# FFN-in units: one of four weight sums moves from VectorE to GpSimd, and its product moves among the plain up tiles

## The chip, the cores and the metric

The kernel runs on 1 core of one Trainium2 chip. The metric is the device time in microseconds (us) of that core, the median of several executions of the same program.

## The reference

One decoder layer on x of 256 tokens by 2048 features, all in float32. The first and the last of its three parts are SwiGLU feed-forward blocks, and the change touches only their input projection:

```
x = x + 0.5 * swiglu_ffn(rmsnorm(x, ffn1_norm), ffn1_w_in, ffn1_w_out)
x = x + concat(attention_A, attention_B) @ w_out        # token mixer, not touched
x = x + 0.5 * swiglu_ffn(rmsnorm(x, ffn2_norm), ffn2_w_in, ffn2_w_out)

def swiglu_ffn(x, w_in, w_out):
    gate, up = jnp.split(x @ w_in, 2, axis=-1)      # w_in: 2048 x 11008, D_FF = 5504
    return (jax.nn.silu(gate) * up) @ w_out
```

## The kernel before

**Tiling.** The input projection of each feed-forward block is cut into 11 units of output columns, ten of 512 gate and 512 up columns and a last one of 384 of each (`UNIT_W`). Unit 0 of each block is computed plainly (`plain_unit`). The other ten of each block, so 20 in all, run `unit(u, j)`; the change touches these and what feeds them.

**What a unit computes.** The 16 row tiles of the weights are used in two ways. Rows 0 to 7 are multiplied plainly: two row tiles are a "half", 128 x 1024 numbers, and the halves are named G0 and G1 (gate) and U0, U1 (up). Rows 8 to 15 of gate and up are handled as a 2 x 2 block product in Strassen-Winograd form: seven products, each of two halves, instead of eight. Four of the seven take their weights from the raw pieces (B11, B21, and so on), and sums of pieces are needed for T1, T3, T2 and T4. The matching sums of the inputs are made once per block in `form_sums`. A product goes into one of four PSUM banks Y, V, Z, X.

**Hi and lo.** Float32 precision is reached with three reduced-precision products: each half of weights is copied by ScalarE (ACT) into `whi`, rounded, and VectorE (DVE) writes the remainder, source minus `whi`, into `wlo`. This pair of steps is `split` (L835 on ACT, L1173 on DVE). TensorE (PE) then runs hi x hi, hi x lo, lo x hi. `whi` and `wlo` are rings of `SLOTS` = 4 halves: ACT may write half h only when PE has used half h - 4 (`weights_used`), DVE may write `wlo` of h when `whi` of h is there (`weights_hi`), and PE starts h when `wlo` of h is there (`weights_lo`).

**Order.** Each engine goes through a list written out by hand. PE's order in a unit is T1, B11, eight transposes of the unit before (`act_turn`), G0, T2, B21, T3, G1, B22, T4, U0, U1; a form product is 2 halves of 6 matmuls, a plain piece 2 halves of 12. The constants `T1, B11, ... U0` are the places of these halves in the unit (22 halves), and U0 stood for all four plain up halves.

**Buffers.** `raw` has 6 slots of 4 row tiles (128 x 2048), filled by one DMA each on SyncE's queue, which waits in order for the slot to come free (`free`, wait on L370). `tsum` is one buffer of the same size. Before the change DVE made four sums in a unit: `sum_t1` (L1335) and `sum_t3` (L1342) near the end of the unit before, `sum_t2` (L1349) over the B11 piece, and `sum_t4` (L1355) into `tsum`, just after the remainder of B21's first half.

**GpSimd (POOL)** only makes a few constants, some small powers (`x_power`, L464, and L495) and a few DMAs.

Of the kernel before, what the change touches and what calls it, by code (L numbers as in the profile page):

```python
# [32 lines left out]
UNITS = -(-D_FF // W)  # L33
# [9 lines left out]

T1, B11, G0, T2, B21, T3, G1, B22, T4, U0 = 0, 2, 4, 6, 8, 10, 12, 14, 16, 18
UNIT_HALVES = 22
# [62 lines left out]
IN_P, OUT_P = [0, 0], [0, 0]  # L108
# [45 lines left out]
def layer(nc, io, out):  # L154
# [3 lines left out]
    with ctx:  # L158
# [144 lines left out]
        def kept(u, g):  # L303
# [19 lines left out]
        xg_ready, s_summed, s_hi, s_ready = (sem(n) for n in ("xg_ready", "s_summed", "s_hi", "s_ready"))  # L323
        sums_done, copied, w_done, gate_added, c11_done = (
            sem(n) for n in ("sums_done", "copied", "w_done", "gate_added", "c11_done"))
        sq_done, hss_ready, hms_ready, hr_ready, hsc_ready, qn_ready, qk_psum, qkT_ready, v_ready = (
# [16 lines left out]
        def _(sp):  # L343
            def free(n):
                for u in range(2):
                    if IN_P[u] <= n < OUT_P[u]:
                        j, i = (n - IN_P[u]) // 8, (n - IN_P[u]) % 8
                        if j == 0:
                            return weights_lo, IN[u] + 2 * i + 2
                        if i == LOAD["B11"]:  # L350
                            return sums_done, 4 * ((UNITS - 1) * u + j)
                        last = {LOAD["B21"]: B21, LOAD["B12"]: T3, LOAD["B22"]: B22, LOAD["G0"]: G0, LOAD["G1"]: G1, LOAD["U0"]: U0, LOAD["U1"]: U0 + 2}[i]
# [97 lines left out]
        def _(pool):  # L450
# [35 lines left out]
            for m in range(2 * GROUPS):  # L486
# [8 lines left out]
                pool.tensor_tensor(hr[:], hms[:], neg_half[:].rearrange("p (b i) -> p b i", b=TB), ALU.pow).then_inc(hr_ready, 1)  # L495
            x_power(2)

        @block.tensor
        def _(pe):
# [87 lines left out]
            def unit(u, j):  # L587
# [238 lines left out]
        def _(act_e):  # L826
# [139 lines left out]
            def unit(u, j):  # L966
                Y, V, Z, X = unit_banks(j)
                base, n, w, s = unit_half(u, j), IN_P[u] + 8 * j, UNIT_W[j], j % 2
                first, w2 = (UNITS - 1) * u + j - 1, 2 * w
                act_e.wait_ge(sums_done, 4 * first + 1)  # L970
                for i in range(2):
# [11 lines left out]
                A(p1s[:, 0:w], Y[:, 0:w], ACT.Copy).then_inc(copied, 1)  # L983
                act_e.wait_ge(sums_done, 4 * first + 3)
                for i in range(2):
                    split(base + T2 + i, piece_half(n + LOAD["B11"], i, w2), w2)
                loaded(n + LOAD["B21"])
# [12 lines left out]
                act_copy(u, j - 1)  # L1000
                act_e.wait_ge(sums_done, 4 * first + 4)
                for i in range(2):
                    split(base + T4 + i, tsum[:, i * w2:(i + 1) * w2], w2)
                loaded(n + LOAD["U0"])
                for i in range(2):
                    split(base + U0 + i, piece_half(n + LOAD["U0"], i, w2), w2)
                loaded(n + LOAD["U1"])
                split(base + U0 + 2, piece_half(n + LOAD["U1"], 0, w2), w2)
                silu(u, j)
                split(base + U0 + 3, piece_half(n + LOAD["U1"], 1, w2), w2)  # L1010

# [156 lines left out]
        def _(dve):  # L1168
# [23 lines left out]
            def form_sums(u):  # L1192
                dve.wait_ge(xg_ready, u + 1)
                A11, A21, A12, A22 = xg[:, 0:4, 0:P], xg[:, 0:4, P:2 * P], xg[:, 4:8, 0:P], xg[:, 4:8, P:2 * P]
                V.tensor_tensor(A22, A21, A22, ALU.add).then_inc(s_summed, 1)
# [4 lines left out]
                V.tensor_tensor(A12, A12, A11, ALU.subtract).then_inc(s_summed, 1)  # L1200

# [127 lines left out]
            def sum_t1(u, j):  # L1329
# [3 lines left out]
                if j > 1:  # L1333
                    dve.wait_ge(weights_lo, unit_half(u, j - 1) + T4 + 2)
                V.tensor_tensor(tsum[:, 0:4 * w], whole(n + LOAD["B12"], w), whole(n + LOAD["B11"], w),  # L1335
                                ALU.subtract).then_inc(sums_done, 1)

            def sum_t3(u, j):
                n, w = IN_P[u] + 8 * j, UNIT_W[j]
                full(n + LOAD["B22"])  # L1340
                dve.wait_ge(sums_done, 4 * ((UNITS - 1) * u + j - 1) + 1)
                V.tensor_tensor(whole(n + LOAD["B12"], w), whole(n + LOAD["B22"], w), whole(n + LOAD["B12"], w),  # L1342
                                ALU.subtract).then_inc(sums_done, 1)

            def sum_t2(u, j):
                n, w = IN_P[u] + 8 * j, UNIT_W[j]
                dve.wait_ge(sums_done, 4 * ((UNITS - 1) * u + j - 1) + 2)
                dve.wait_ge(weights_lo, unit_half(u, j) + B11 + 2)
                V.tensor_tensor(whole(n + LOAD["B11"], w), whole(n + LOAD["B12"], w), whole(n + LOAD["B11"], w),  # L1349
                                ALU.add).then_inc(sums_done, 1)  # L1350

            def sum_t4(u, j):
                n, w = IN_P[u] + 8 * j, UNIT_W[j]
                dve.wait_ge(sums_done, 4 * ((UNITS - 1) * u + j - 1) + 3)
                V.tensor_tensor(tsum[:, 0:4 * w], whole(n + LOAD["B21"], w), whole(n + LOAD["B11"], w),  # L1355
                                ALU.subtract).then_inc(sums_done, 1)

# [32 lines left out]
            def unit(u, j):  # L1390
# [11 lines left out]
                for i in range(2):  # L1402
                    split(base + T2 + i, piece_half(n + LOAD["B11"], i, w2), w2)
# [12 lines left out]
                split(base + T4, tsum[:, 0:w2], w2)  # L1416
# [3 lines left out]
                split(base + T4 + 1, tsum[:, w2:2 * w2], w2)  # L1420
                split(base + U0, piece_half(n + LOAD["U0"], 0, w2), w2)
                dve.wait_ge(weights_used, base + B22 + 2)
                dve.wait_ge(copied, 3 * first + 3)
                V.tensor_tensor(gset[:, s, 0, 0:w], Z[:, 0:w], gset[:, s, 0, 0:w], ALU.add).then_inc(gate_added, 1)
                split(base + U0 + 1, piece_half(n + LOAD["U0"], 1, w2), w2)
                split(base + U0 + 2, piece_half(n + LOAD["U1"], 0, w2), w2)
                if j + 1 < UNITS:
                    sum_t1(u, j + 1)
                split(base + U0 + 3, piece_half(n + LOAD["U1"], 1, w2), w2)
                if j + 1 < UNITS:  # L1430
# [253 lines left out]
```

## Time and profile before

| what | value |
|---|---|
| median of 3 runs | 1762.78 us (1762.37 to 1762.95) |
| span of the profiled execution | 1760.7 us |
| PE busy | 1754.5 us |
| DVE busy | 1490.9 us |
| ACT busy | 1077.5 us |
| POOL busy | 28.1 us |
| matmuls | 8036 |

The span runs from the first to the last instruction of the profiled execution. It is 2.1 us under the median of the runs. No time of its own is shown for the profiled execution beside its span. Matmuls overlap in the record, so that PE's busy time hides waits shorter than the pipeline's own length; start-to-start distances are the surer measure.

### The profile page before, as it was taken

How to read it: one execution, taken by the hardware profiler on the slowest of the kernel's cores; microseconds unless marked ns; L12 is line 12 of the kernel's file. 1: busy time of each engine (PE TensorE's matmuls, PEld its weight loads, DVE VectorE, ACT ScalarE, POOL GpSimd, SP SyncE). 2: the span in 40 equal slices, each digit the busy share in tenths (PEclk: the TensorE clock that was granted, in tenths of full speed). 3: DMA queues.
4: the chain of work that ended last, by engine and by line, in shares of the span. 5: the costliest groups of instructions: out<-in, count | busy, mean ns of one | idle time of the engine just before them, and what ended most of it. 6: DMA issues, size and time to landing. Idle time of an engine off the chain costs nothing.

```text
span 1760.7 us, 20876 instructions
## 1 busy us (share of the span) xinstructions
PE 1754.5 (100%) x8036; PEld 1463.4 (83%) x8036; DVE 1490.9 (85%) x1627; ACT 1077.5 (61%) x1359; POOL 28.1 (2%) x34
## 2 busy tenths in 40 slices
PE   9999999999999999999999999999999999999999
PEld 7888888888988888888888888888888888988887
DVE  7999999998899998575655655999999999899998
ACT  7666666666666666454545544666666666666665
POOL 0000000000000001100000000000000000000000
PEclk9999999999999999999999999999999999999999
DMA  9655555554655556555455547355555555564762
GB/s 379 233 213 211 196 191 192 191 191 156 228 215 192 203 215 209 182 188 182 156 188 166 169 168 262 121 211 194 202 213 212 213 213 192 190 207 163 257 212 93
DMA packets 154931, 350.85 MB, mean 199 GB/s; under 512 B 5864, under 2 KB 14592, under 8 KB 154704
## 3 DMA queue, kind: packets, MB, share of 16 engines
q1 hardware_dynamic: 152288, 342.02, 54.9%
q0 software_dynamic: 1424, 5.53, 1.0%
q10 hardware_dynamic: 1120, 1.97, 0.3%
q8 instruction: 64, 1.05, 0.2%
q14 instruction: 35, 0.29, 0.0%
HBM read 347.37 MB, written 3.69 MB: 199 GB/s over the span
## 4 chain that ended last, share of the span: by engine, by line
PE 95%; DVE 2%; SPq 1%; DMA 1%; issue 0%; ACT 0%; ACTq 0%; DVEq 0%
PE bank L570 9%; PE bank L568 9%; PE bank L569 9%; PE bank L552 7%; PE bank L554 7%; PE bank L553 7%; PE bank L509 7%; PE bank L511 7%; PE bank L510 7%; PE bank L639 5%; PE bank L641 5%; PE bank L640 5%; PE bank L667 3%; PE bank L666 3%; PE bank L665 3%; PE bank L537 1%
## 5 line engine op out<-in xcount | busy, mean ns | idle before, releaser
L1173 DVE TENSOR_TENSOR wlo<-raw,whi 128x1024 fp32r<-128x1024 f32 (+1 forms) x626 | 742.1, 1205 | 176.9 <-ACT whi L835 171.8
L835 ACT ACTIVATE whi<-raw 128x1024 fp32r<-128x1024 f32 (+1 forms) x626 | 650.7, 1046 | 392.8 <-PE bank L511 188.9
L568 PE MATMUL bank<-whi,xs 128*128 128x512 f32 (+1 forms) x768 | 297.9, 388 | 0.5 <-DVE xs L1368 0.2
L570 PE MATMUL bank<-whi,xs 128*128 128x512 f32 (+1 forms) x768 | 295.5, 385 | 0.0
L569 PE MATMUL bank<-wlo,xs 128*128 128x512 f32 (+1 forms) x768 | 295.4, 385 | 0.0
L568 PEld LDWEIGHTS bank<-whi,xs 128*128 128x128 f32 x768 | 144.3, 188 | 29.0 <-DVE wlo L1365 1.1
L570 PEld LDWEIGHTS bank<-whi,xs 128*128 128x128 f32 x768 | 144.2, 188 | 27.7
L569 PEld LDWEIGHTS bank<-wlo,xs 128*128 128x128 f32 x768 | 144.4, 188 | 26.8
L639 PE MATMUL bank<-whi,aw_hi 128*128 128x512 f32 x420 | 164.0, 390 | 0.0
L641 PE MATMUL bank<-whi,aw_lo 128*128 128x512 f32 x420 | 163.5, 389 | 0.0
L640 PE MATMUL bank<-wlo,aw_hi 128*128 128x512 f32 x420 | 163.5, 389 | 0.0
L509 PE MATMUL bank<-whi,xs 128*128 128x512 f32 x384 | 155.1, 404 | 0.4 <-DVE wlo L1173 0.4
L511 PE MATMUL bank<-whi,xs 128*128 128x512 f32 x384 | 150.0, 391 | 0.0
L510 PE MATMUL bank<-wlo,xs 128*128 128x512 f32 x384 | 149.5, 389 | 0.0
L835 ACT ACTIVATE whi<-tsum 128x1024 fp32r<-128x1024 f32 (+1 forms) x80 | 83.0, 1040 | 97.8 <-PE bank L570 64.1
L552 PE MATMUL bank<-whi,sf 128*128 128x512 f32 (+1 forms) x320 | 122.8, 384 | 0.0
L554 PE MATMUL bank<-whi,sf 128*128 128x512 f32 (+1 forms) x320 | 122.8, 384 | 0.0
L553 PE MATMUL bank<-wlo,sf 128*128 128x512 f32 (+1 forms) x320 | 122.7, 384 | 0.0
L1037 ACT ACTIVATE whi<-raw 128x1024 fp32r<-128x1024 f32 x80 | 84.8, 1060 | 61.9 <-PE bank L641 38.6
L1173 DVE TENSOR_TENSOR wlo<-tsum,whi 128x1024 fp32r<-128x1024 f32 (+1 forms) x80 | 94.0, 1195 | 26.0 <-ACT whi L835 26.0
L1453 DVE TENSOR_TENSOR wlo<-raw,whi 128x1024 fp32r<-128x1024 f32 x80 | 97.1, 1220 | 1.7 <-ACT whi L1037 0.8
L639 PEld LDWEIGHTS bank<-whi,aw_hi 128*128 128x128 f32 x420 | 78.8, 188 | 17.4 <-issue 1.3
(204 smaller groups left out, 2724.7 us busy)
## 6 DMA issues: line engine op xcount, KB each, us to landing
raw<-ffn_w_in SPq DMA_DIRECT2D x158, 1024.0 KB, 7.1
raw<-ffn_w_out SPq DMA_DIRECT2D x84, 1024.0 KB, 6.7
raw<-w_in SPq DMA_DIRECT2D x48, 1024.0 KB, 5.0
raw<-w_out SPq DMA_DIRECT2D x16, 1024.0 KB, 5.0
raw<-ffn_w_in SPq DMA_DIRECT2D x16, 768.0 KB, 4.5
x<-x SPq DMA_DIRECT2D x4, 512.0 KB, 12.4
raw<-ffn_w_out SPq DMA_DIRECT2D x4, 512.0 KB, 3.8
raw<-ffn_w_in SPq DMA_DIRECT2D x3, 512.0 KB, 7.4
```

What stands on the lines that cost most here:

```text
L509: mm(banks[b][:, 0:w], stationary[:, k, 0, tok], hi, start=k == 0, stop=False, skip_group_check=True)
L510: mm(banks[b][:, 0:w], stationary[:, k, 0, tok], lo, start=False, stop=False, skip_group_check=True)
L511: last = mm(banks[b][:, 0:w], stationary[:, k, 1, tok], hi, start=False, stop=k == k_total - 1, skip_group_check=True)
L552: mm(bank_out[:, 0:w], st_hi, hi, start=start and i == 0 and k == 0, stop=False, skip_group_check=True)
L568: mm(banks[b][:, 0:w], xs[:, k + i, 0, tok], hi, start=starts[b] and k + i == 0, stop=False, skip_group_check=True)
L569: mm(banks[b][:, 0:w], xs[:, k + i, 0, tok], lo, start=False, stop=False, skip_group_check=True)
L570: last = mm(banks[b][:, 0:w], xs[:, k + i, 1, tok], hi, start=False, stop=k + i == last_k, skip_group_check=True)
L639: mm(bank_out[:], st_hi, hi, start=i == 0, stop=False, skip_group_check=True)
L640: mm(bank_out[:], st_hi, lo, start=False, stop=False, skip_group_check=True)
L641: last = mm(bank_out[:], st_lo, hi, start=False, stop=k == FT - 1, skip_group_check=True)
L835: A(whi[:, h % SLOTS, 0:n_el], src, ACT.Copy).then_inc(weights_hi, 1)
L1173: V.tensor_tensor(wlo[:, h % SLOTS, 0:n_el], src, whi[:, h % SLOTS, 0:n_el].bitcast(f32), ALU.subtract).then_inc(weights_lo, 1)
```

## The change

`sum_t4` is gone from DVE. GpSimd makes the same sum with a new function `add_b21`: it waits until DVE has written the remainder of B21's second half, and then adds the raw B21 piece onto `tsum` in place (128 x 2048 float32, two inputs in SBUF), which now holds T2 at that time: `sum_t2` writes into `tsum` instead of over the B11 piece, and the T2 halves are split from there. ACT waits for `t4_added` before it copies T4. The T4 product and its splits move behind the first two plain up halves (U0) and ahead of the last two (U1). The B11 slot comes free after `sum_t2`, the B21 slot after the add. For T4 to be a plain addition, some signs are turned in the sums of inputs, the sums of weights and in two additions onto PSUM banks; the number and shape of those instructions stay.

```diff
-T1, B11, G0, T2, B21, T3, G1, B22, T4, U0 = 0, 2, 4, 6, 8, 10, 12, 14, 16, 18
+T1, B11, G0, T2, B21, T3, G1, B22, U0, T4, U1 = 0, 2, 4, 6, 8, 10, 12, 14, 16, 18, 20
...
                         if i == LOAD["B11"]:
-                            return sums_done, 4 * ((UNITS - 1) * u + j)
+                            return sums_done, 3 * ((UNITS - 1) * u + j)
+                        if i == LOAD["B21"]:
+                            return t4_added, (UNITS - 1) * u + j
...
+            def add_b21(u, j):
+                n = 4 * UNIT_W[j]
+                pool.wait_ge(weights_lo, unit_half(u, j) + B21 + 2)
+                pool.tensor_tensor(tsum[:, 0:n], tsum[:, 0:n], raw[:, raw_slot(IN_P[u] + 8 * j + LOAD["B21"]), 0:n],
+                                   ALU.add).then_inc(t4_added, 1)
+
+            for j in range(1, UNITS):
+                add_b21(0, j)
...
             x_power(2)
+            for j in range(1, UNITS):
+                add_b21(1, j)
...
         # PE, unit
                 pe.wait_ge(w_done, first + 1)
+                for i in range(2):
+                    plain(base + U0 + i, 2 * i, (V, Y), (False, False), w, -1)
                 form(base + T4, Y, lambda k, t: xs[:, 12 + k, t, blk1], w, False)
-                for i in range(4):
-                    plain(base + U0 + i, 2 * i, (V, Y), (False, False), w, 7)
+                for i in range(2):
+                    plain(base + U1 + i, 4 + 2 * i, (V, Y), (False, False), w, 7)
...
         # ACT, unit
-                act_e.wait_ge(sums_done, 4 * first + 4)
+                loaded(n + LOAD["U0"])
+                for i in range(2):
+                    split(base + U0 + i, piece_half(n + LOAD["U0"], i, w2), w2)
+                act_e.wait_ge(t4_added, first + 1)
                 for i in range(2):
                     split(base + T4 + i, tsum[:, i * w2:(i + 1) * w2], w2)
...
         # DVE
-                V.tensor_tensor(whole(n + LOAD["B11"], w), whole(n + LOAD["B12"], w), whole(n + LOAD["B11"], w),
+                V.tensor_tensor(tsum[:, 0:4 * w], whole(n + LOAD["B12"], w), whole(n + LOAD["B11"], w),
                                 ALU.add).then_inc(sums_done, 1)
-
-            def sum_t4(u, j):
-                n, w = IN_P[u] + 8 * j, UNIT_W[j]
-                dve.wait_ge(sums_done, 4 * ((UNITS - 1) * u + j - 1) + 3)
-                V.tensor_tensor(tsum[:, 0:4 * w], whole(n + LOAD["B21"], w), whole(n + LOAD["B11"], w),
-                                ALU.subtract).then_inc(sums_done, 1)
...
                 split(base + B21, piece_half(n + LOAD["B21"], 0, w2), w2)
-                sum_t4(u, j)
                 split(base + B21 + 1, piece_half(n + LOAD["B21"], 1, w2), w2)
...
-                V.tensor_tensor(gset[:, s, 1, 0:w], Y[:, 0:w], gset[:, s, 1, 0:w], ALU.add).then_inc(w_done, 1)
+                V.tensor_tensor(gset[:, s, 1, 0:w], gset[:, s, 1, 0:w], Y[:, 0:w], ALU.subtract).then_inc(w_done, 1)
```

## Rows read from the trace of the kernel before

**Rows 1.** The page's busy times, share of the span, instructions.
```profile
PE 1754.5 (100%) x8036; PEld 1463.4 (83%) x8036; DVE 1490.9 (85%) x1627; ACT 1077.5 (61%) x1359; POOL 28.1 (2%) x34
```

**Rows 2.** Windows of one unit each: busy us per engine, TensorE clock, DMA share.
```profile
69.40:111.12 41.72, 41.72 (x190) 34.61 (x189) 38.56 (x33) 26.80 (x30) 0.00 (x0) 1.00 0.57 203
...
361.40:403.10 41.70, 41.70 (x190) 34.62 (x189) 38.50 (x33) 26.81 (x30) 0.00 (x0) 1.00 0.56 202
```

**Rows 3.** Timeline of PE in one unit: start us, duration us, instruction.
```profile
278.38 0.39 PE L552 MATMUL bank<-whi,sf 128*128 128x512 f32 x1
...
279.74 0.39 PE L552 MATMUL bank<-whi,sf 128*128 128x512 f32 x1
...
294.70 0.39 PE L568 MATMUL bank<-whi,xs 128*128 128x512 f32 x1
...
302.86 0.39 PE L552 MATMUL bank<-whi,sf 128*128 128x512 f32 x1
```

**Rows 4.** Timeline of DVE in the same unit.
```profile
267.86 4.94 DVE L1173 TENSOR_TENSOR wlo<-raw,whi 128x1024 fp32r<-128x1024 f32 x4
272.72 2.28 DVE L1355 TENSOR_TENSOR tsum<-raw 128x2048 f32<-128x2048 f32 x1
274.92 2.35 DVE L1173 TENSOR_TENSOR wlo<-raw,whi 128x1024 fp32r<-128x1024 f32 x2
277.44 3.50 DVE L1173 TENSOR_TENSOR wlo<-raw,whi 128x1024 fp32r<-128x1024 f32 x3 [0.17 <-ACT whi L835]
...
298.81 2.35 DVE L1173 TENSOR_TENSOR wlo<-tsum,whi 128x1024 fp32r<-128x1024 f32 x2
```

**Rows 5.** Timeline of ACT in the same unit.
```profile
273.14 1.06 ACT L835 ACTIVATE whi<-raw 128x1024 fp32r<-128x1024 f32 x1 [1.60 <-PE bank L570]
274.50 1.06 ACT L835 ACTIVATE whi<-raw 128x1024 fp32r<-128x1024 f32 x1 [0.29 <-PE bank L554]
```

**Rows 6.** POOL's groups by form: busy us, mean ns of one, idle before.
```profile
L455 POOL TENSOR_SCALAR_AFFINE_SELECT ident<-ident 128x128 f32<-128x128 f32 x1 | 0.3, 292 | 0.2 <-POOL ident L453 0.2
L453 POOL MEMSET ident<- 128x128 f32 x1 | 0.2, 206 | 0.0
...
L452 POOL MEMSET warm<- 128x1 f32 x1 | 0.1, 99 | 0.0
```

**Rows 7.** Timeline of POOL: three of its eleven powers.
```profile
708.57 0.72 POOL L464 TENSOR_TENSOR rstd<-xms,neg_half 128x2 f32<-128x2 f32 x1 [28.86 <-DVE xms L1211]
...
743.55 1.66 POOL L495 TENSOR_TENSOR hr<-hms,neg_half 128x8 f32<-128x8 f32 x1 [2.33 <-DVE hms L1484]
...
1112.50 1.60 POOL L464 TENSOR_TENSOR rstd<-xms,neg_half 128x2 f32<-128x2 f32 x1 [145.30 <-DVE xms L1211]
```

**Rows 8.** Timeline of DVE around these three POOL instructions.
```profile
709.70 1.23 DVE L1173 TENSOR_TENSOR wlo<-raw,whi 128x1024 fp32r<-128x1024 f32 x1 [1.22 <-ACT whi L835]
...
743.60 1.23 DVE L1173 TENSOR_TENSOR wlo<-raw,whi 128x1024 fp32r<-128x1024 f32 x1
...
1112.33 1.22 DVE L1173 TENSOR_TENSOR wlo<-raw,whi 128x1024 fp32r<-128x1024 f32 x1
```

**Rows 9.** Timelines of PE, ACT and DVE in a block's last, 384 wide unit.
```profile
442.12 0.33 PE L552 MATMUL bank<-whi,sf 128*128 128x384 f32 x1
...
438.68 0.85 ACT L835 ACTIVATE whi<-raw 128x768 fp32r<-128x768 f32 x1 [0.19 <-PE bank L554]
...
446.90 0.96 DVE L1173 TENSOR_TENSOR wlo<-tsum,whi 128x768 fp32r<-128x768 f32 x1 [0.73 <-ACT whi L835]
```

**Rows 10.** Waits of the DMA queue: us in total, times, longest us.
```profile
SPq L370 <- DVE tsum L1355: 389.8, 20, 20.5
```

**Rows 11.** Timeline of SyncE's queue: loads issued near the unit's end.
```profile
284.29 12.79 SPq L370 DMA_DIRECT2D raw<-ffn_w_in  x6
```

**Rows 12.** Timeline of PE: transposes at the start, and in a unit.
```profile
1.60 4.53 PE L517 MATMUL bank<-ident 128*128 128x128 f32 x20 [1.60 <-POOL ident L455]
...
266.58 1.04 PE L537 MATMUL bank<-ident,gset 128*128 128x128 f32 x8
```

More of the change, by code:

```diff
@@ L323, in layer @@
         xg_ready, s_summed, s_hi, s_ready = (sem(n) for n in ("xg_ready", "s_summed", "s_hi", "s_ready"))
-        sums_done, copied, w_done, gate_added, c11_done = (
-            sem(n) for n in ("sums_done", "copied", "w_done", "gate_added", "c11_done"))
+        sums_done, t4_added, copied, w_done, gate_added, c11_done = (
+            sem(n) for n in ("sums_done", "t4_added", "copied", "w_done", "gate_added", "c11_done"))
         sq_done, hss_ready, hms_ready, hr_ready, hsc_ready, qn_ready, qk_psum, qkT_ready, v_ready = (
@@ L350, in free @@
                         if i == LOAD["B11"]:
-                            return sums_done, 4 * ((UNITS - 1) * u + j)
-                        last = {LOAD["B21"]: B21, LOAD["B12"]: T3, LOAD["B22"]: B22, LOAD["G0"]: G0, LOAD["G1"]: G1, LOAD["U0"]: U0, LOAD["U1"]: U0 + 2}[i]
+                            return sums_done, 3 * ((UNITS - 1) * u + j)
+                        if i == LOAD["B21"]:
+                            return t4_added, (UNITS - 1) * u + j
+                        last = {LOAD["B12"]: T3, LOAD["B22"]: B22, LOAD["G0"]: G0, LOAD["G1"]: G1, LOAD["U0"]: U0, LOAD["U1"]: U1}[i]
                         return weights_lo, unit_half(u, j) + last + 2
@@ L969, in unit @@
                 first, w2 = (UNITS - 1) * u + j - 1, 2 * w
-                act_e.wait_ge(sums_done, 4 * first + 1)
+                act_e.wait_ge(sums_done, 3 * first + 1)
                 for i in range(2):
@@ L983, in unit @@
                 A(p1s[:, 0:w], Y[:, 0:w], ACT.Copy).then_inc(copied, 1)
-                act_e.wait_ge(sums_done, 4 * first + 3)
+                act_e.wait_ge(sums_done, 3 * first + 3)
                 for i in range(2):
-                    split(base + T2 + i, piece_half(n + LOAD["B11"], i, w2), w2)
+                    split(base + T2 + i, tsum[:, i * w2:(i + 1) * w2], w2)
                 loaded(n + LOAD["B21"])
@@ L1000, in unit @@
                 act_copy(u, j - 1)
-                act_e.wait_ge(sums_done, 4 * first + 4)
-                for i in range(2):
-                    split(base + T4 + i, tsum[:, i * w2:(i + 1) * w2], w2)
                 loaded(n + LOAD["U0"])
@@ L1006, in unit @@
                     split(base + U0 + i, piece_half(n + LOAD["U0"], i, w2), w2)
+                act_e.wait_ge(t4_added, first + 1)
+                for i in range(2):
+                    split(base + T4 + i, tsum[:, i * w2:(i + 1) * w2], w2)
                 loaded(n + LOAD["U1"])
-                split(base + U0 + 2, piece_half(n + LOAD["U1"], 0, w2), w2)
+                split(base + U1, piece_half(n + LOAD["U1"], 0, w2), w2)
                 silu(u, j)
-                split(base + U0 + 3, piece_half(n + LOAD["U1"], 1, w2), w2)
+                split(base + U1 + 1, piece_half(n + LOAD["U1"], 1, w2), w2)
             def ffn_out(u):
@@ L1194, in form_sums @@
                 A11, A21, A12, A22 = xg[:, 0:4, 0:P], xg[:, 0:4, P:2 * P], xg[:, 4:8, 0:P], xg[:, 4:8, P:2 * P]
-                V.tensor_tensor(A22, A21, A22, ALU.add).then_inc(s_summed, 1)
+                V.tensor_tensor(A22, A21, A22, ALU.subtract).then_inc(s_summed, 1)
                 dve.wait_ge(s_summed, 4 * u + 1)
@@ L1199, in form_sums @@
                 dve.wait_ge(s_summed, 4 * u + 3)
-                V.tensor_tensor(A12, A12, A11, ALU.subtract).then_inc(s_summed, 1)
+                V.tensor_tensor(A12, A12, A11, ALU.add).then_inc(s_summed, 1)
             def form_splits(u):
@@ L1335, in sum_t1 @@
                 V.tensor_tensor(tsum[:, 0:4 * w], whole(n + LOAD["B12"], w), whole(n + LOAD["B11"], w),
-                                ALU.subtract).then_inc(sums_done, 1)
+                                ALU.add).then_inc(sums_done, 1)
             def sum_t3(u, j):
@@ L1340, in sum_t3 @@
                 full(n + LOAD["B22"])
-                dve.wait_ge(sums_done, 4 * ((UNITS - 1) * u + j - 1) + 1)
+                dve.wait_ge(sums_done, 3 * ((UNITS - 1) * u + j - 1) + 1)
                 V.tensor_tensor(whole(n + LOAD["B12"], w), whole(n + LOAD["B22"], w), whole(n + LOAD["B12"], w),
-                                ALU.subtract).then_inc(sums_done, 1)
+                                ALU.add).then_inc(sums_done, 1)
             def sum_t2(u, j):
                 n, w = IN_P[u] + 8 * j, UNIT_W[j]
-                dve.wait_ge(sums_done, 4 * ((UNITS - 1) * u + j - 1) + 2)
+                dve.wait_ge(sums_done, 3 * ((UNITS - 1) * u + j - 1) + 2)
                 dve.wait_ge(weights_lo, unit_half(u, j) + B11 + 2)
-                V.tensor_tensor(whole(n + LOAD["B11"], w), whole(n + LOAD["B12"], w), whole(n + LOAD["B11"], w),
+                V.tensor_tensor(tsum[:, 0:4 * w], whole(n + LOAD["B12"], w), whole(n + LOAD["B11"], w),
                                 ALU.add).then_inc(sums_done, 1)
-            def sum_t4(u, j):
-                n, w = IN_P[u] + 8 * j, UNIT_W[j]
-                dve.wait_ge(sums_done, 4 * ((UNITS - 1) * u + j - 1) + 3)
-                V.tensor_tensor(tsum[:, 0:4 * w], whole(n + LOAD["B21"], w), whole(n + LOAD["B11"], w),
-                                ALU.subtract).then_inc(sums_done, 1)
             def plain_unit(u):
@@ L1402, in unit @@
                 for i in range(2):
-                    split(base + T2 + i, piece_half(n + LOAD["B11"], i, w2), w2)
+                    split(base + T2 + i, tsum[:, i * w2:(i + 1) * w2], w2)
                 split(base + B21, piece_half(n + LOAD["B21"], 0, w2), w2)
-                sum_t4(u, j)
                 split(base + B21 + 1, piece_half(n + LOAD["B21"], 1, w2), w2)
@@ L1412, in unit @@
                 dve.wait_ge(copied, 3 * first + 1)
-                V.tensor_tensor(gset[:, s, 1, 0:w], Y[:, 0:w], gset[:, s, 1, 0:w], ALU.add).then_inc(w_done, 1)
+                V.tensor_tensor(gset[:, s, 1, 0:w], gset[:, s, 1, 0:w], Y[:, 0:w], ALU.subtract).then_inc(w_done, 1)
                 for i in range(2):
                     split(base + B22 + i, piece_half(n + LOAD["B22"], i, w2), w2)
-                split(base + T4, tsum[:, 0:w2], w2)
+                split(base + U0, piece_half(n + LOAD["U0"], 0, w2), w2)
                 dve.wait_ge(weights_used, base + G1 + 2)
@@ L1419, in unit @@
                 V.tensor_tensor(gset[:, s, 1, 0:w], X[:, 0:w], gset[:, s, 1, 0:w], ALU.add).then_inc(gate_added, 1)
-                split(base + T4 + 1, tsum[:, w2:2 * w2], w2)
-                split(base + U0, piece_half(n + LOAD["U0"], 0, w2), w2)
+                split(base + U0 + 1, piece_half(n + LOAD["U0"], 1, w2), w2)
+                split(base + T4, tsum[:, 0:w2], w2)
                 dve.wait_ge(weights_used, base + B22 + 2)
                 dve.wait_ge(copied, 3 * first + 3)
-                V.tensor_tensor(gset[:, s, 0, 0:w], Z[:, 0:w], gset[:, s, 0, 0:w], ALU.add).then_inc(gate_added, 1)
-                split(base + U0 + 1, piece_half(n + LOAD["U0"], 1, w2), w2)
-                split(base + U0 + 2, piece_half(n + LOAD["U1"], 0, w2), w2)
+                V.tensor_tensor(gset[:, s, 0, 0:w], Z[:, 0:w], gset[:, s, 0, 0:w], ALU.subtract).then_inc(gate_added, 1)
+                split(base + T4 + 1, tsum[:, w2:2 * w2], w2)
+                split(base + U1, piece_half(n + LOAD["U1"], 0, w2), w2)
                 if j + 1 < UNITS:
                     sum_t1(u, j + 1)
-                split(base + U0 + 3, piece_half(n + LOAD["U1"], 1, w2), w2)
+                split(base + U1 + 1, piece_half(n + LOAD["U1"], 1, w2), w2)
                 if j + 1 < UNITS:
```

## The prediction

> **What bounds the kernel now.** I read the page's busy times first. PE is busy for 1754.5 of 1760.7 us [rows 1]; a thing taken off another engine can win only where PE waits for it. Then the windows, one unit each: eight units in a row of 41.7 us, PE busy through all of each, granted clock 1.00 (2.4 GHz), DVE busy 38.5 and ACT 26.8 [rows 2]. Then PE's timeline in one unit: the two halves of T3 start 1.36 us apart, which is 6 matmuls of 0.227 us [rows 3], and a whole unit is 180 such matmuls (14 form halves of 6, 8 plain halves of 12) and eight transposes: 180 x 0.227 = 40.9, and 0.8 for the transposes. That is all of the 41.7 us. So PE never waits in a unit; it has nothing to win there. DVE is next, with 3.2 us idle in a unit, and what counts is how far it runs ahead of PE at each half.
>
> **How far ahead, at the place of the edit.** Before, DVE writes four remainders from 267.86, sum_t4 from 272.72 to 274.92 (in line the instructions follow 0.08 us before the shown end), the remainders of B21's second and T3's first half from 274.92, T3's second from 277.44 [rows 4]. T3's halves are due on PE at 278.38 and 279.74 [rows 3]. The first is ready at 274.92 + 2.35 = 277.3, 1.1 us early; the second at 277.44 + 1.2 = 278.65, 1.1 us early. This is the thinnest lead of the stretch, as the halves behind T3 are plain ones, for which PE takes 2.7 us and DVE 1.15.
>
> **The parts of the change.**
>
> Removed: 20 sums of 2.28 us on DVE (18 of this size and 2 of 384-wide units). PE waits for none of them, so this is worth 0 us by itself. It makes DVE earlier only up to the next wait for ACT: `whi` of B21's second half is ready at 273.14 + 1.06 = 274.20, of T3's first at 275.56, and of T3's second only when DVE's own wait for it ends, 277.44 [rows 4, 5], so DVE writes B21's second remainder from 274.23 to 275.45, T3's first from 275.59 to 276.8 and T3's second at 277.44 as before. ACT's times hang on the ring and so on PE.
>
> T2 written to `tsum`: the same instruction with another output, 0. The signs: the same instructions, 0. The B11 slot comes free earlier, after sum_t2 at 267.86 and not after sum_t4 at 274.92; the DMA queue waited 389.8 us for it in 20 units [rows 4, 10], but what it lets in is U0, and had anyone on PE's path waited for U0, units would show a gap [rows 2]; 0. The B21 slot now waits for the add; the piece that takes it goes out in the burst of loads from 284.29 on [rows 11], so an add that ends by then costs nothing.
>
> T4 moved: it is due at 294.70 instead of 289.26, as U0's two plain halves go first [rows 3]. A place in the ring behind them comes free at most 1.36 us later, one form half, for U1's first half, and with it `sum_t1` and the next unit's first remainder: this was ready at 298.81 + 1.2 = 300.0 for 302.86 [rows 3, 4], 2.9 us early, so 1.4 us are covered: 0. If the shift were more than 2.9 us, the rest would be paid 20 times.
>
> Added: an addition on POOL, 128 x 2048, two SBUF inputs. The trace has no POOL instruction of this size. Nearest rows: memset of one column 99 ns, of 128 columns 206, a select with one input over 128 columns 292 [rows 6]. A written element costs (206 - 99)/127 = 0.84 ns and an input (292 - 206)/128 = 0.67 ns more. Two inputs: 0.84 + 2 x 0.67 = 2.18 ns, times 2048, and 0.1 to start: 4.57 us. From below I take DVE's own 2.28 us for this sum [rows 4], from above two passes at the select's whole rate of 1.5 ns: 6.2 us. The powers, 0.72 and 1.66 us for 2 and 8 elements [rows 7], would give far more, but a power is computed, not moved, and I leave them out. I take 4.6. The Trainium skill, GPSIMD Engine Reference, section on performance versus the Vector engine, gives 4497 ns as measured for this very operation; by it the sum below would be 2 us smaller, as an estimate. The value itself is no problem for T4: it starts at 275.55, ends at 280.1, and T4's copy can be made once B22's first half has left the ring: 294.70 less two plain halves of 2.72 and a form half of 1.36, 287.9.
>
> What matters is DVE beside it. POOL's two-element power took 0.72 us with DVE idle until 709.70, but 1.60 us at 1112.50, when DVE had begun a remainder (two SBUF inputs) at 1112.33 that ended at 1113.55; 1113.5 + 0.6 is just its end [rows 7, 8]. So a POOL instruction that reads SBUF stood still until the DVE instruction with two SBUF inputs was over. I read this as a shared path that one holds to the end of its reading. The other order the trace shows only for a tiny read: at 743.60 DVE started 0.05 us after an eight-element POOL read and lost 0.01 us. I take it that the rule holds there too, and that the add keeps the path for its whole 4.6 us. The Trainium skill, SBUF — State Buffer, section "Who interferes with whom", says this outright: a VectorE instruction with two SBUF inputs and a GpSimd instruction that reads SBUF exclude each other, whichever starts first keeps the port pair for the whole instruction, and the other "fully blocks". The trace agrees in the one order it shows; by the rows alone, where only POOL is seen to stand, the sum could as well be 0.
>
> **Worked out for one unit.** POOL starts at about 275.55, between B21's second remainder (ends 275.45) and T3's first (hi part ready at 275.56). It holds until 275.55 + 4.57 = 280.1; T3's first remainder is then ready at 280.1 + 1.22 + 0.05 = 281.4, and PE wanted it at 278.38: 3.0 us of waiting. If DVE is first, T3's first is ready in time, POOL holds from 276.8 to 281.4, and T3's second is ready at 282.6 for 279.74: 2.9. Behind it DVE catches up at 1.15 us a half against 1.36 and then 2.7. Queued behind the held instruction on DVE are the remainders of G1 and the addition onto the Y bank; they are late by as much as PE is, so nobody waits twice. So 18 x 3.0 = 54. In the 384-wide unit T3 is due at 442.12, its hi part is ready at 439.53, the add takes 0.1 + 1536 x 2.18 = 3.45: 439.55 + 3.45 + 0.96 + 0.05 - 442.12 = 1.9 [rows 9], twice: 4. Together **+58 us** on the profiled span of 1760.7, so 1819; the runs' median is 2.1 above that span, so **1821 us**.
>
> The bounds of the add: with 2.28 us the wait is 275.55 + 2.28 + 1.27 - 278.38 = 0.7, in the narrow units 0.2, sum 13: 1776. With 6.2 us it is 4.6, narrow (4.7 us) 3.1, sum 89: 1852.
>
> **Rivals.**
>
> No change (1762.8). The path is not shared this way, or VectorE always goes first and POOL takes what is left; its sum has until 294.70 less 2.3 for the two copies of T4's first half, 292, some 16 us. For it: the eight-element read cost DVE nothing, and DVE's sums disappear. Against it: the 1.60 us row. This is the rival on the other side. The point from which it decides: a hold of DVE shorter than 278.38 - 275.55 - 1.27 = 1.55 us costs nothing, a longer one costs what it is longer.
>
> Both go at half speed while they overlap. T3's first remainder 275.6 to 277.9, its second to 280.2 (0.5 late), G1's first to 282.5 (0.9 more late): 1.4 x 20 = 27, so 1790 us. Only the 1.60 row speaks against it, which is a full stop.
>
> The clock falls after each wait. All rows of units show 1.00, but PE never waits there. At the start, after 1.6 us without work, 20 transposes take 4.53 us, 0.23 each, and in a unit eight take 1.04, 0.13 each [rows 12], so PE began at about the lower of its levels (1.2 GHz). If each new wait were followed by such a stretch, 4.5 us at half speed lose 2.2, times 20 is 45 more: about 1866. PE is idle 1.6 us there without work behind it, here 2.9 us after a full stretch; no row shows what that does.
>
> Faster would need waits of PE in the units, and the rows of units show none.
>
> **Chances.** Full stop of DVE 0.70, with its own range 1776 to 1852; half speed 0.09; no change 0.15; clock 0.04; faster 0.02. Faster by over 0.2% (3.5 us, about what a measurement of this kernel can tell from none) 0.02, within it 0.15, slower 0.83. The range holds the stop, the half speed and the lower end of the clock case (a shorter slow stretch), 0.8 in all: 1770 to 1855. It leaves out no change and faster below, and the rest of the clock case above.
>
> **What the profile will show.** POOL: 20 additions of 4.6 us (3.5 in the narrow units). DVE: one L1173 instruction a unit, just behind B21's, of over 4 us or begun over 4 us late. PE: one wait of 3.0 us a unit, for `wlo`, at T3's first or second half; units of 44.7 us. T4's copy on ACT without a wait for POOL. Wrong if units keep 41.7 us, if the add takes over 6 us, if the wait stands at T4 or T1, or if the granted clock falls under 1.00.

## The result, and the profile after

The changed kernel takes 1843.51 us (median of 4, 1837.4 to 1845.95) against 1762.72 before, a ratio of 1.0453 (95% interval 1.0441 to 1.0466): 81 us slower. Forecast were 1821 us and a range of 1770 to 1855. The span of the profiled execution is 1839.8 us, 79.1 more than before.

The page's busy times and the waits of PE (us in total, times, longest) in the changed kernel:

```profile
PE 1777.9 (97%) x8036; PEld 1473.9 (80%) x8036; DVE 1531.0 (83%) x1607; ACT 1076.3 (59%) x1359; POOL 118.4 (6%) x54
...
PE bank L565 <- DVE wlo L1188: 54.8, 20, 2.8
```

Before, PE had nowhere a wait of this kind worth a row. Now there is one in each of the 20 units, at the first matmul of a form product (L565), for a remainder of DVE. DVE has 20 instructions less (1607 for 1627) and is 40 us longer busy. Where that comes from, the groups by form and the timelines of GpSimd and DVE in one unit say:

```profile
L478 POOL TENSOR_TENSOR tsum<-tsum,raw 128x2048 f32<-128x2048 f32 x18 | 82.5, 4582 | 703.1 <-DVE wlo L1188 703.1
...
L1188 DVE TENSOR_TENSOR wlo<-raw,whi 128x1024 fp32r<-128x1024 f32 x554 | 747.6, 1363 | 228.3 <-ACT whi L850 223.3
L1188 DVE TENSOR_TENSOR wlo<-tsum,whi 128x1024 fp32r<-128x1024 f32 x108 | 128.8, 1220 | 3.5 <-ACT whi L850 3.5
...
251.89 4.58 POOL L478 TENSOR_TENSOR tsum<-tsum,raw 128x2048 f32<-128x2048 f32 x1 [43.10 <-DVE wlo L1188]
...
250.58 10.38 DVE L1188 TENSOR_TENSOR wlo<-raw,whi 128x1024 fp32r<-128x1024 f32 x5 [1.32 <-ACT whi L850]
```

GpSimd's add takes 4.58 us, where 4.57 was worked out. The mean remainder from `raw` rose from 1.22 to 1.36 us, that from `tsum` stayed. The last row holds five remainders in a row: at 1.14 us apart they would be 5.8 us long, and they are 10.4, so they are 4.6 us longer in all, as long as GpSimd's add, which begins at 251.89, just behind the first of them (250.58 + 1.22 = 251.80). PE in the same unit:

```profile
254.50 0.39 PE L567 MATMUL bank<-whi,xs 128*128 128x512 f32 x1
257.70 0.76 PE L565 MATMUL bank<-whi,sf 128*128 128x512 f32 x1 [2.81 <-DVE wlo L1188]
258.26 0.63 PE L566 MATMUL bank<-wlo,sf 128*128 128x512 f32 x1
258.69 0.63 PE L567 MATMUL bank<-whi,sf 128*128 128x512 f32 x1
...
395.16 0.47 PE L565 MATMUL bank<-whi,sf 128*128 128x512 f32 x1 [2.81 <-DVE wlo L1188]
395.47 0.40 PE L566 MATMUL bank<-wlo,sf 128*128 128x512 f32 x1
```

The next matmul was due at 254.50 + 0.23 = 254.73 and began at 257.70, 2.97 us late; this is T3's first half, where [rows 3] had no gap. Behind the wait two things can be seen. At 395.16 the matmuls go on at nearly their usual distance. Behind 257.70 they are 0.43 us apart, not 0.23. The windows from the start of one add to the start of the next, called distances from here on, and four short ones around that wait, show what it is (the last three numbers are granted clock, DMA share and GB/s):

```profile
112.93:157.77 44.84, 42.03 (x190) 34.53 (x189) 40.51 (x31) 26.78 (x30) 4.58 (x1) 1.00 0.53 187
204.21:251.89 47.68, 44.87 (x190) 36.61 (x189) 40.59 (x31) 26.77 (x30) 4.58 (x2) 0.93 0.50 176
251.89:298.05 46.16, 43.35 (x190) 35.50 (x189) 40.59 (x31) 26.78 (x30) 4.58 (x2) 0.96 0.51 182
...
256.00:258.00 2.00, 0.30 (x1) 0.33 (x2) 2.00 (x2) 0.00 (x0) 0.47 (x1) 0.77 0.00 0
258.00:259.00 1.00, 1.00 (x3) 0.81 (x3) 1.00 (x2) 0.00 (x0) 0.00 (x0) 0.50 0.00 0
259.00:260.00 1.00, 1.00 (x4) 0.71 (x4) 1.00 (x2) 0.00 (x0) 0.00 (x0) 0.50 0.31 43
260.00:261.00 1.00, 1.00 (x5) 0.82 (x4) 0.96 (x1) 0.31 (x1) 0.00 (x0) 0.75 0.72 178
```

The granted clock is at 0.50, the lower level of 1.2 GHz. Cut finer, the windows give 0.59 from 257.0 to 257.5 and 0.99 from 260.5 to 261.0: the clock fell at about 257.1, when PE had stood since 254.89, and rose at about 260.5. From 257.70 on PE worked in that stretch, at half its pace. A unit of 512 columns was 41.72 us; it is 44.84 now where the clock stays at 1.00, and mostly 46.2 to 46.5, once 47.7, where it falls. There are 18 distances inside the two blocks, 16 from one wide unit to the next and 2 that end in the narrow one (43.61 and 41.99 us). In 11 of the 18 the granted clock falls, and these are 18 us longer in sum than without it. So the 79 us are 18 x 3.12 = 56 us of waits in the wide units, 18 us of clock, and what is left, about 5, in the two narrow ones.

### The profile page after: what moved, and what is told of

Its sections match the earlier page's. It is cut to its first block, busy times and chain, and to the rows that moved or that the text cites. A ratio compares the mean times of both kernels' runs of the same rounds, so it can differ in the third digit from the quotient of the medians.

```text
span 1839.8 us, 20876 instructions
## 1 busy us (share of the span) xinstructions
PE 1777.9 (97%) x8036; PEld 1473.9 (80%) x8036; DVE 1531.0 (83%) x1607; ACT 1076.3 (59%) x1359; POOL 118.4 (6%) x54
## 3 DMA queue, kind: packets, MB, share of 16 engines
q8 instruction: 64, 1.05, 0.2%
## 4 chain that ended last, share of the span: by engine, by line
PE 91%; DVE 7%; ACT 1%; DMA 0%; issue 0%; SPq 0%; ACTq 0%; DVEq 0%
PE bank L581 9%; PE bank L582 9%; PE bank L583 9%; DVE wlo L1188 6%; PE bank L522 6%; PE bank L524 6%; PE bank L523 6%; PE bank L565 6%; PE bank L567 6%; PE bank L566 6%; PE bank L654 5%; PE bank L655 5%; PE bank L656 5%; PE bank L680 3%; PE bank L681 3%; PE bank L682 3%
## 5 line engine op out<-in xcount | busy, mean ns | idle before, releaser
L1188 DVE TENSOR_TENSOR wlo<-raw,whi 128x1024 fp32r<-128x1024 f32 (+1 forms) x586 | 783.5, 1351 | 237.8 <-ACT whi L850 232.6
L850 ACT ACTIVATE whi<-raw 128x1024 fp32r<-128x1024 f32 (+1 forms) x586 | 611.1, 1047 | 520.4 <-PE bank L583 203.3
L565 PE MATMUL bank<-whi,sf 128*128 128x512 f32 (+1 forms) x320 | 130.8, 409 | 54.8 <-DVE wlo L1188 54.8
L850 ACT ACTIVATE whi<-tsum 128x1024 fp32r<-128x1024 f32 (+1 forms) x120 | 120.6, 1036 | 50.8 <-DVE tsum L1350 20.5
L1188 DVE TENSOR_TENSOR wlo<-tsum,whi 128x1024 fp32r<-128x1024 f32 (+1 forms) x120 | 139.9, 1193 | 3.9 <-ACT whi L850 3.5
L478 POOL TENSOR_TENSOR tsum<-tsum,raw 128x2048 f32<-128x2048 f32 (+1 forms) x20 | 90.3, 4514 | 779.5 <-DVE wlo L1188 779.5
L567 PE MATMUL bank<-whi,sf 128*128 128x512 f32 (+1 forms) x320 | 129.9, 406 | 0.0
L566 PE MATMUL bank<-wlo,sf 128*128 128x512 f32 (+1 forms) x320 | 129.2, 404 | 0.0
L565 PEld LDWEIGHTS bank<-whi,sf 128*128 128x128 f32 x320 | 63.4, 198 | 74.4 <-issue 60.2
```

The lines of the kernel that those rows point to most:

```text
L565: mm(bank_out[:, 0:w], st_hi, hi, start=start and i == 0 and k == 0, stop=False, skip_group_check=True)
L850: A(whi[:, h % SLOTS, 0:n_el], src, ACT.Copy).then_inc(weights_hi, 1)
L1188: V.tensor_tensor(wlo[:, h % SLOTS, 0:n_el], src, whi[:, h % SLOTS, 0:n_el].bitcast(f32), ALU.subtract).then_inc(weights_lo, 1)
```

## The experiments

In all of them the times stand beside the kernel before on the same chip (1762.7 to 1762.9). In the code lines, "..." marks what is left out. The runs with an extra GpSimd instruction work over the B21 piece when nobody reads it any more and compute what the kernel before computes.

**All but GpSimd's add.** The changed kernel, the sum made by VectorE in its old place:

```diff
...
-            for j in range(1, UNITS):
-                add_b21(0, j)
...
+                V.tensor_tensor(tsum[:, 0:4 * w], tsum[:, 0:4 * w], whole(n + LOAD["B21"], w),
+                                ALU.add).then_inc(t4_added, 1)
...
                 split(base + B21, piece_half(n + LOAD["B21"], 0, w2), w2)
+                sum_t4(u, j)
                 split(base + B21 + 1, piece_half(n + LOAD["B21"], 1, w2), w2)
...
```

> The changed kernel in all its parts (T2 in tsum, T4 behind U0, turned signs, B11 slot freed early), only that VectorE makes the sum T2 + B21 at its old place and GpSimd makes none. Theory (the whole loss is VectorE standing still behind GpSimd's add, and the clock that falls with PE's waits): units of 41.7 us as before, granted clock 1.00, 1763 us within 2. Rival 1 (the move of T4 or the later sum of the next unit's T1 costs a wait of its own): a wait of PE at T4, U1 or T1 and more than 1767 us. Rival 2 (the early issue of U0's load disturbs): longer remainders or copies in the stretch of the load, again over 1767.

Measured: 1763.52 us, ratio 1.0004 (0.9995 to 1.0013), clock 1.00. The move of T4, T2 in `tsum`, the signs and the earlier slot cost nothing that can be measured. All of the loss belongs to having the add on GpSimd, at its place.

**Only GpSimd's add, with nobody waiting for it.**

```diff
+            def ghost(u, j):
+                b21 = raw[:, raw_slot(IN_P[u] + 8 * j + LOAD["B21"]), :]
+                pool.wait_ge(weights_lo, unit_half(u, j) + B21 + 2)
+                n = min(2048, 4 * UNIT_W[j])
+                pool.tensor_tensor(b21[:, 0:n], b21[:, 0:n], b21[:, 0:n], ALU.add).then_inc(ghost_done, 1)
...
```

> The kernel before, unchanged, with one more GpSimd addition in each of the 20 units, 128 x 2048 with two SBUF inputs, made when B21's second remainder is written, over the B21 piece, which nobody reads any more; only the slot's next load waits for it. No engine on PE's path waits for its result. Theory (VectorE is shut out of the second SBUF read path while GpSimd reads): one VectorE remainder in each unit late by up to 4.6 us, PE waits about 3.2 us in each unit (T3's second half: path held from 277.25 to 281.8, ready at 283.0, due at 279.74), 18 x 3.2 + 2 x 2 = 62 us, and up to 20 to 30 us of lower clock as in the changed kernel: 1825 to 1855. Rival (the loss comes from waiting for the sum's result, or from where T4 stands): 1763.

Measured: 1815.46 us, ratio 1.0299 (1.0285 to 1.0313). The rival, that the loss hangs on the sum's result or T4's place, is out: here nothing on PE's path waits for GpSimd. But the time lies below what I expected, 1825 at least. Distances between wide units are 43.97 us where the clock stays and 45.6 in four of the 16; a fifth fall, to 0.96 in the window, is in the first block's distance that ends in the narrow unit (42.64 us against 40.99 in the second). Without a fall PE waits 2.25 us a unit and not 3.2, so the path was held for 3.6 us (277.2 + 3.6 + 1.2 = 282.0, 2.25 after 279.74), though the record of the add says 4.51. That opened the question that the last two runs answer.

**GpSimd busy, but reading nothing.** Three memsets in place of the add:

```diff
+                for k in range(3):
+                    if k:
+                        pool.wait_ge(ghost_step, 2 * first + k)
+                    pool.memset(b21[:, 0:4 * UNIT_W[j]], 0.0).then_inc(ghost_done if k == 2 else ghost_step, 1)
...
```

> As the run with the extra addition, but GpSimd writes zeros three times over the same piece (three memsets of 128 x 2048, each about 1.8 us, so about 5.4 us of GpSimd work that writes SBUF and reads nothing). Theory (it is GpSimd's reading that shuts VectorE's second input out): no remainder is longer than 1.23 us, units of 41.7 us, 1763 within 2. Rival (any GpSimd work beside VectorE stops it, through the write path or the whole port pair): waits of PE of up to 3 us a unit, over 1800.

Measured: 1762.69 us, ratio 0.9999 (0.999 to 1.0008). The timelines of GpSimd and DVE in one unit:

```profile
234.69 5.57 POOL L482 MEMSET raw<- 128x2048 f32 x3 [36.15 <-DVE wlo L1189]
...
235.94 3.50 DVE L1189 TENSOR_TENSOR wlo<-raw,whi 128x1024 fp32r<-128x1024 f32 x3 [0.16 <-ACT whi L851]
```

5.6 us of GpSimd's writing, and three remainders within it take 3.50 us as in [rows 4]. So it is GpSimd's reading that shuts VectorE out. The memsets write to the place to which the extra add writes, so the write and its address are not what counts; whether the address of what is read does, was not tried.

**A short add.** The extra addition once more, cut down:

```diff
-                n = min(2048, 4 * UNIT_W[j])
+                n = min(512, 4 * UNIT_W[j])
```

> As the run with the extra addition, but only 128 x 512, so that GpSimd reads for about 1.2 us. Theory (what counts is how far the hold exceeds VectorE's lead over PE): the path is held from about 277.25 to 278.45, T3's second remainder is ready at 279.7 for 279.74, so no wait or under 0.1 us: 1763 to 1765. Rival (each collision costs a fixed restart, whatever the size): more than 1770.

Measured: 1763.40 us, ratio 1.0002 (0.9993 to 1.0011). The collision is there, the three remainders take 4.09 us and not 3.50:

```profile
236.15 4.09 DVE L1186 TENSOR_TENSOR wlo<-raw,whi 128x1024 fp32r<-128x1024 f32 x3 [0.16 <-ACT whi L848]
```

A hold of about 1 us at a place where DVE is 1.1 us ahead costs nothing; there is no fixed price per collision.

**VectorE late, GpSimd idle.** The real sum moved behind B21's second remainder, and one more sum behind it:

```diff
...
+                V.tensor_tensor(tsum[:, 0:4 * w], tsum[:, 0:4 * w], whole(n + LOAD["B21"], w),
+                                ALU.add).then_inc(t4_added, 1)
+                dve.wait_ge(t4_added, 2 * ((UNITS - 1) * u + j - 1) + 1)
+                V.tensor_tensor(whole(n + LOAD["B21"], w), whole(n + LOAD["B21"], w), whole(n + LOAD["B22"], w),
+                                ALU.add).then_inc(t4_added, 1)
...
                 split(base + B21 + 1, piece_half(n + LOAD["B21"], 1, w2), w2)
+                sum_t4(u, j)
...
```

> The changed kernel with GpSimd idle: VectorE makes the sum T2 + B21 itself, but only after B21's second remainder, and behind it one more sum of 128 x 2048 over the dead B21 piece, so that T3's first remainder starts about 4.4 us late, as behind GpSimd's add. Question: is the loss beyond 3 us a unit, the lower granted clock, a thing of PE's waiting or of GpSimd's work? Theory (PE's wait of about 3 us lets the clock fall in some units): PE waits 2.8 us a unit, clock 0.5 for some us behind the wait in about half of the units, 54 us of waits and 10 to 25 of clock, 1827 to 1843. Rival (the clock falls because of GpSimd's add): units of 44.5 us all through, clock 1.00, 1818.

Measured: 1842.77 us, ratio 1.0454 (1.0435 to 1.0472), within the spread of the changed kernel itself. Two windows of one unit each:

```profile
158.37:203.11 44.74, 42.01 (x189) 34.55 (x189) 40.52 (x35) 26.78 (x30) 0.00 (x0) 1.00 0.52 189
294.89:341.20 46.31, 43.58 (x189) 35.68 (x188) 40.60 (x34) 26.79 (x30) 0.00 (x0) 0.96 0.50 182
```

With GpSimd at 0.00 the units are 44.7 us, 3.0 more than before, and in 11 of 18 distances the clock falls, to 0.96 or less in the window, as often as in the changed kernel. So the clock falls behind PE's waits whoever makes PE wait, and the rival, that GpSimd's work lowers it, is out.

**Half as late.** The same without the extra sum:

```diff
                 split(base + B21 + 1, piece_half(n + LOAD["B21"], 1, w2), w2)
+                sum_t4(u, j)
```

> As the run with VectorE late and GpSimd idle, but with the real sum alone behind B21's second remainder and no second one, so that T3's first remainder starts 2.2 us late instead of 4.4. Theory (PE waits for what exceeds VectorE's lead, and a short wait leaves the clock): ready at 275.45 + 2.2 + 1.2 = 278.9 for 278.38, 0.5 us a unit, 10 us, clock 1.00: 1773 (1768 to 1776). Rival (any wait at this place costs clock too): over 1780 and a granted clock under 0.99 in windows of some units.

Measured: 1776.94 us, ratio 1.0080 (1.0065 to 1.0095); units of 42.4 us, the wide ones all within 0.06 us of each other, clock 1.00. The wait is 0.7 us and not the expected 0.5, so the time is 1 us over the expected range; the wait costs just itself, 14 us. The rival, that any wait at this place costs clock too, is out. The sum costs these 14 us by its place alone: on the same engine, one remainder earlier, it is free (1763.52).

**The real add in four slices.**

```diff
...
-                pool.wait_ge(weights_lo, unit_half(u, j) + B21 + 2)
-                pool.tensor_tensor(tsum[:, 0:n], tsum[:, 0:n], raw[:, raw_slot(IN_P[u] + 8 * j + LOAD["B21"]), 0:n],
-                                   ALU.add).then_inc(t4_added, 1)
...
+                for k, h in enumerate((B21 + 2, G1 + 1, G1 + 2, B22 + 2)):
+                    part = slice(k * w, (k + 1) * w)
+                    pool.wait_ge(weights_lo, unit_half(u, j) + h)
+                    pool.tensor_tensor(tsum[:, part], tsum[:, part], b21[:, part], ALU.add).then_inc(t4_added, 1)
...
```

> The changed kernel with the same real sum on GpSimd cut into four additions of 128 x 512, each let go by another remainder of VectorE (B21's second, G1's first and second, B22's second). Each holds the read path about 1.2 us, and VectorE's lead at these places is 1.5, 2.9, 3.4 and about 1.8 us. Theory (a hold shorter than the lead costs nothing): no wait of PE, 1763 to 1765. Rival (the added holds pile up, 4.9 us in a unit in which VectorE has only 5.4 us idle): 10 us and more above, with waits at T3, G1 or T1.

Measured: 1763.56 us, ratio 1.0005 (0.9996 to 1.0014). Same sum, same engine, same amount of reading, and no wait of PE behind it. The first row is the window of one unit, the second and third are VectorE and GpSimd in it:

```profile
238.88:280.63 41.75, 41.75 (x190) 34.62 (x189) 38.76 (x32) 26.80 (x30) 7.97 (x5) 1.00 0.55 202
...
240.53 5.03 DVE L1190 TENSOR_TENSOR wlo<-raw,whi 128x1024 fp32r<-128x1024 f32 x3
...
275.90 1.29 POOL L481 TENSOR_TENSOR tsum<-tsum,raw 128x512 f32<-128x512 f32 x1 [29.18 <-DVE wlo L1190]
```

VectorE stands here too: its three remainders take 5.03 us and not 3.50, in pieces that its lead over PE covers. A slice's own work is about 1.2 us, as in the one record of 1.29 us; the other three records of a unit are some 2.2 us, with the slice's own standing behind VectorE in them.

It repairs the change but does not win over the kernel before, since PE is busy through the unit in both.

**The whole add, later.**

```diff
-                pool.wait_ge(weights_lo, unit_half(u, j) + B21 + 2)
+                pool.wait_ge(weights_lo, unit_half(u, j) + G1 + 2)
```

> The changed kernel with one edit: GpSimd's add waits for G1's second remainder instead of B21's second. It then holds the path from 281.05 to 285.65 in the unit's time, over the addition onto the Y bank (one input in PSUM, should not be held) and B22's first remainder, ready then at 286.9 for 286.54. Theory: PE waits about 0.4 us a unit at B22's first half, 8 us in all, clock 1.00, 1771 (1766 to 1775). If the addition with one input in PSUM is held too, it starts 4 us late, without cost for PE. Rival (the add costs its 4.6 us of VectorE wherever it stands): over 1800.

Measured: 1783.39 us, ratio 1.0118 (1.0102 to 1.0133): far below the changed kernel, but 20 us above the one before, 12 more than I had worked out. GpSimd and DVE in one unit, and from the list of waits the one that is new:

```profile
202.83 4.63 POOL L478 TENSOR_TENSOR tsum<-tsum,raw 128x2048 f32<-128x2048 f32 x1 [39.05 <-DVE wlo L1188]
...
203.12 0.69 DVE L1421 TENSOR_TENSOR gset<-gset,bank 128x512 f32<-128x512 f32 x1 [0.37 <-PE bank L567]
203.72 7.08 DVE L1188 TENSOR_TENSOR wlo<-raw,whi 128x1024 fp32r<-128x1024 f32 x3
...
DVE tsum L1350 <- DMA raw<-ffn_w_in: 12.1, 17, 1.9
```

The addition with one input in PSUM runs inside GpSimd's hold at its usual 0.69 us. B22's first remainder behind it is held. PE waits only about 0.2 us there. But the B22 piece's slot comes free only with its last remainder, and the queue of loads waits for it in order; `sum_t1` now waits for a load 17 times, which it did not in the changed kernel, and the next unit's first halves pay: units of 42.4 to 42.6 us, and four in the first block of 43.7 to 44.0. What I had left out was who else waits for the held instruction. Why only four units pay the larger price was not tried.

**One input instead of two.** A GpSimd copy in place:

```diff
-                pool.tensor_tensor(b21[:, 0:n], b21[:, 0:n], b21[:, 0:n], ALU.add).then_inc(ghost_done, 1)
+                pool.tensor_copy(b21[:, 0:n], b21[:, 0:n]).then_inc(ghost_done, 1)
```

> The kernel before with an extra GpSimd copy in each unit, 128 x 2048 in place over the dead B21 piece: one SBUF input instead of two. By the rate of the select it takes some 3.2 us. Theory (any GpSimd instruction that reads SBUF holds the read path for as long as it reads): T3's second remainder late by about 3, PE waits up to 1.9 us a unit, up to 36 us, 1780 to 1800. Rival (only two-input GpSimd instructions fill the path, one input leaves room for VectorE): 1763.

Measured: 1774.28 us, ratio 1.0065 (1.0051 to 1.0079). A one-input read excludes VectorE too; the rival is out. The time is below the expected 1780 to 1800, since the copy was faster than I took it for; GpSimd and DVE in one unit:

```profile
237.22 2.83 POOL L479 COPY raw<-raw 128x2048 f32<-128x2048 f32 x1 [39.45 <-DVE wlo L1186]
...
235.94 2.35 DVE L1186 TENSOR_TENSOR wlo<-raw,whi 128x1024 fp32r<-128x1024 f32 x2
238.46 4.94 DVE L1186 TENSOR_TENSOR wlo<-raw,whi 128x1024 fp32r<-128x1024 f32 x3 [0.17 <-ACT whi L848]
```

The record begins at 237.22, but the second of DVE's two remainders is in the path until about 238.15, 0.93 us longer. The copy ends at 240.05 and so holds for 1.9 us, 0.88 ns an element; DVE's next three take 4.94 instead of 3.50, 1.4 us of standing still, and PE waits 0.55 us a unit.

**Equal and different inputs, 128 x 1024.** The extra addition with n = 1024 and equal inputs, and then with two halves of the piece:

```diff
...
+                n = 2 * UNIT_W[j]
+                pool.tensor_tensor(b21[:, 0:n], b21[:, 0:n], b21[:, n:2 * n], ALU.add).then_inc(ghost_done, 1)
...
```

> The kernel before with an extra GpSimd addition in each unit, 128 x 1024, both inputs the same piece. In the run with 2048 the wait of PE was 2.25 us a unit, which is a hold of 3.6 us, and GpSimd's record of 4.51 us began 0.9 us before VectorE's running remainder ended. Theory A (GpSimd reads faster when both inputs are the same addresses, some 1.74 ns an element): hold 1.9 us, record 2.8 us, PE waits 0.55 us a unit, 11 us, 1774. Theory B (the rate is 2.19 ns as in the changed kernel, but GpSimd gets through a part of its work while VectorE still runs): record 2.3 us, and waits of PE as with two different inputs.

> As the run with the extra addition of 128 x 1024, but the second input is the other half of the piece, as in a real sum. Theory A: hold 0.1 + 1024 x 2.19 = 2.3 us, record 3.2 us, PE waits 277.2 + 2.3 + 1.25 - 279.74 = 1.0 us a unit, 20 us, 1783. Theory B: the same time as with equal inputs, within 1 us.

Measured: 1774.90 us (ratio 1.0069, 1.0052 to 1.0086) with equal inputs, 1784.16 us (1.0122, 1.0107 to 1.0137) with different ones. GpSimd's groups, first of the one, then of the other:

```profile
L479 POOL TENSOR_TENSOR raw<-raw 128x1024 f32<-128x1024 f32 x20 | 55.6, 2780 | 748.4 <-DVE wlo L1186 748.4
```

```profile
L479 POOL TENSOR_TENSOR raw<-raw 128x1024 f32<-128x1024 f32 x18 | 59.9, 3326 | 675.5 <-DVE wlo L1186 675.5
```

The single records of wide units are 2.81 and 3.33 us. Less some 0.93 us behind DVE's running remainder, as worked out for the copy, 1.9 and 2.4 us of work are left. Theory A holds to within 1.2 us in both totals, and B, which wants equal times, is out by 9 us: two reads of the same addresses take some 1.74 ns an element, two different ones 2.2. That is why the run with 2048 equal inputs came out lower than expected.

## Why the prediction was right, and where it was off

**PE is saturated, so nothing can be gained.** Right: with all of the change but GpSimd's part the ratio is 1.0004, though DVE's sum was still there; and with the sum gone from DVE and sliced on GpSimd it is 1.0005. The 2.28 us a unit taken off DVE are worth nothing.

**T4's move, `tsum`, signs, slots: 0.** Right, by the same two runs. T4's copy nowhere waited for GpSimd.

**The add takes 4.6 us.** Right, 4.58 (the 4497 ns that the prediction named beside its sum are 2% less), but the way there was partly luck: I had taken 0.84 ns for a written element and 0.67 for each input. A one-input copy needs 0.88 in all and two different inputs 2.19, so inputs do not add up in equal steps. The sum of my steps, 2.18, hit by chance.

**It shuts VectorE out for its whole length, once a unit.** Right, and shown from both sides: with nobody waiting for the add the loss is there, with a memset in its place it is not, with VectorE delayed by its own work the same time results without GpSimd. The row of 1.60 us in [rows 7], where GpSimd stood behind VectorE, could only show one order; the runs show the other. The Trainium skill, SBUF — State Buffer, "Who interferes with whom", states the exclusion; its words on the whole instruction and the full block stand at VectorE's two-port modes, and the runs here show the same for two SBUF inputs. Each of its exceptions that a run here touches holds: a GpSimd instruction that only writes (1762.69 us) and a VectorE instruction with one SBUF input (0.69 us within a hold) do not collide.

**3.0 us of waiting a unit at T3.** Right: 2.97 us at T3's first half, GpSimd first; 3.12 a unit by the distances. VectorE was first only in the narrow unit of the first block, where the add's record is 4.31 us for 3.48 in the second, and the case worked out for it (2.9 us) asks for nearly the same. Waits in sum some 61 us, where 58 were forecast. "Half speed" is out: five remainders came 4.6 us late, where half speed through the add's 4.6 us would make it 2.3.

**No loss of clock.** This is the term that was mis-sized. The forecast had 0 for it in its sum and gave it a chance of 0.04, as an event of every unit, worth 45 us. It came in 11 of 18 distances and was worth 18 us, nearly all of the 22 us between 1821 and 1843.5. By the prediction's own list of signs this was one of being wrong: it named a granted clock under 1.00, and units of 44.7 us for what are mostly 46.2 to 46.5. The row of transposes at the start [rows 12] did show PE at half pace after idleness; a forecast of 3 us waits should have carried a part of it. That row alone could not prove the clock: the windows show 1.00 there too, but the trace's record of the clock begins only 6.9 us into the span, where the matmuls come to their usual distance.

## What to carry to other kernels

Before work is given to GpSimd, look at what VectorE does beside it: while a GpSimd instruction reads SBUF, a VectorE instruction with two SBUF inputs stands still, and here the hold was as long as the whole GpSimd instruction (4.6 us for 128 x 2048). Cut it into pieces shorter than VectorE's lead at each place, and let each go behind an instruction after which there is such a lead; four slices of about 1.2 us each were free where one add of 4.6 cost 81 us. In this kernel a wait of the saturated PE cost more than its length once it was long: those of 0.5 to 1.05 us cost only themselves, those of 3.1 us a third more.

## What the runs showed of the hardware that was not expected

The clock's answer to waits depends on their length, and behind waits of one length it falls in some units and not in others. Excess per unit of 0.7 us (the sum once late on VectorE): no distance with a lower clock. 1.05 us (1024 different inputs): none either, wide units of 42.8 us, all within 0.05. 2.25 us: 5 of 18. 3.0 to 3.1 us: 11 of 18 behind GpSimd, 11 of 18 behind VectorE. A fall costs 1.3 to 1.7 us, 2.8 to 2.9 in the longest. It is not shown to be chance: with 2.25 us it comes in every fourth unit of a block, and all four runs of that kernel have a mean clock of 0.995. What decides which unit is hit was not tried. The falls go with the wider spread of runs, 8.6 us in the changed kernel against 0.6 before: its fastest run has a mean clock of 0.993, its slowest one of 0.986.

GpSimd adds a piece to itself faster, 1.74 ns an element, than two different pieces, 2.19, so an extra instruction made for a measurement must read what the real one reads. What sets the two rates was not tried.
